# Another order for the first round of the gated layers, and for the loop over attention heads

## The reference

```
u = rms_norm_2(x, norm_w) @ w_in
z_a, xbc, dt_raw, q_b, k_b, v_b, gate_lr, g_b = split_cols(u, EVEN_SPLITS)
xbc = silu(causal_depthwise_conv(xbc, conv_w, conv_b))
...
y_diag = einsum('bcgeij,bcjgep->bcigep', cb[:, :, :, None] * decay_ij, xdt)
y = y_diag + y_off + d_skip[:, :, None] * x_c          # ssd_chunked_scan
y_a = rms_norm_2(y_a * silu(z_a), ssd_norm_w)
...
scores = einsum('bnihd,bnjhd->bnhij', q * exp(gcs - ref), k * exp(ref - gcs))
chunk_kv = einsum('bnjhd,bnjhv->bnhdv', k * exp(g_last[:, :, None] - gcs), v)
o_b = rms_norm_2(gla_chunked(q_b, k_b, v_b, log_decay), gla_norm_w) * silu(g_b)
x = x + concatenate([y_a, o_b]) @ w_out
...
o = moba_attention(q, k, v) * silu(z)                  # softmax attention
x = x + o @ w_out
```

## Time and profile before

| | us |
|---|---|
| median of 3 runs | 868.39 (868.36 to 868.85) |
| the profiled execution | 868.39 |
| its span | 866.6 |
| PE busy | 841.5 (97%) |
| DVE busy | 613.7 (71%) |
| ACT busy | 490.8 (57%) |
| POOL busy | 145.1 (17%) |

### The profile page before, as it was taken

The page is one execution under the profiler, slowest core; times in us unless marked ns, Lnnn a source line. Parts: engine busy times, 40 slices in busy tenths (PEclk is TensorE's granted clock), DMA queues, the critical chain, the costliest instruction groups (busy, mean ns, idle before and its releaser), DMA issues.

```text
span 866.6 us, 16776 instructions
## 1 busy us (share of the span) xinstructions
PE 841.5 (97%) x6768; PEld 803.8 (93%) x6768; DVE 613.7 (71%) x1004; ACT 490.8 (57%) x814; POOL 145.1 (17%) x151
## 2 busy tenths in 40 slices
PE   7999999999999999999999999789999999999996
PEld 6999999999999989999999999789999999888886
DVE  6647787886666686767764478797887697568754
ACT  6345556445444565555564458558777555346654
POOL 0000000000000333333341121335434011000002
PEclk9999999999999999999999999899999999999998
DMA  9654424436666524665566624435544376654431
GB/s 338 210 153 128 158 98 158 135 112 180 192 178 190 175 87 155 194 187 181 174 193 215 191 82 155 163 124 176 183 147 154 115 217 184 186 171 143 123 98 49
DMA packets 39853, 139.81 MB, mean 161 GB/s; under 512 B 4432, under 2 KB 5600, under 8 KB 39648
## 3 DMA queue, kind: packets, MB, share of 16 engines
q1 hardware_dynamic: 37728, 135.71, 49.8%
q10 hardware_dynamic: 2048, 3.02, 1.0%
HBM read 137.65 MB, written 1.06 MB: 160 GB/s over the span
## 4 chain that ended last, share of the span: by engine, by line
PE 79%; DVE 12%; ACT 4%; POOL 3%; issue 1%; DMA 1%; DVEq 0%; SPq 0%; ACTq 0%; POOLq 0%
PE ps L1593 62%; PE ps L1596 5%; DVE weights_lo L984 4%; PE ps L1618 3%; PE ps L1690 1%; DVE arena L1204 1%; DVE arena L1176 1%; PE ps L1680 1%; POOL arena L441 1%; PE ps L1705 1%; PE ps L1960 1%; PE ps L1942 1%; DMA raw_weights<-weights_in 1%; DVE x_lo L1171 1%; POOL arena L462 1%
## 5 line engine op out<-in xcount | busy, mean ns | idle before, releaser
L1593 PE MATMUL ps<-x_hi,weights_hi 128*128 128x256 f32 (+3 forms) x1288 | 374.5, 291 | 6.3 <-DVE x_lo L999 2.8
L984 DVE TENSOR_TENSOR weights_lo<-raw_weights,weights_hi 128x1024 fp32r<-128x1024 f32 x252 | 311.7, 1241 | 92.9 <-ACT weights_hi L549 92.8
L1593 PE MATMUL ps<-x_lo,weights_hi 128*128 128x256 f32 (+3 forms) x1288 | 364.6, 283 | 0.0
L1593 PE MATMUL ps<-x_hi,weights_lo 128*128 128x256 f32 (+3 forms) x1288 | 364.1, 283 | 0.0
L549 ACT ACTIVATE weights_hi<-raw_weights 128x1024 fp32r<-128x1024 f32 x252 | 264.8, 1053 | 163.5 <-issue 71.0
L1593 PEld LDWEIGHTS ps<-x_hi,weights_hi 128*128 128x128 f32 x1288 | 244.1, 190 | 14.3 <-issue 7.0
L1593 PEld LDWEIGHTS ps<-x_lo,weights_hi 128*128 128x128 f32 x1288 | 244.3, 190 | 1.0 <-issue 0.7
L1593 PEld LDWEIGHTS ps<-x_hi,weights_lo 128*128 128x128 f32 x1288 | 244.4, 190 | 0.0
L1593 PE MATMUL ps<-y_hi,weights_hi 128*128 128x256 f32 (+1 forms) x488 | 137.8, 282 | 1.4 <-POOL y_lo L445 1.4
L1593 PE MATMUL ps<-y_lo,weights_hi 128*128 128x256 f32 (+1 forms) x488 | 137.4, 282 | 0.0
L1593 PE MATMUL ps<-y_hi,weights_lo 128*128 128x256 f32 (+1 forms) x488 | 137.1, 281 | 0.0
(11 more groups left out here) (230 smaller groups left out, 1075.0 us busy)
## 6 DMA issues: line engine op xcount, KB each, us to landing
raw_weights<-weights_in SPq DMA_DIRECT2D x252, 512.0 KB, 3.7
arena<-decay_rows ACTq DMA_DIRECT2D x8, 256.0 KB, 3.9
masks<-masks_in SPq DMA_DIRECT2D x1, 1379.0 KB, 11.0
hidden<-xT_in SPq DMA_DIRECT2D x2, 272.0 KB, 3.6
hidden<-xT_in SPq DMA_DIRECT2D x1, 544.0 KB, 6.2
raw_weights<-weights_in SPq DMA_DIRECT2D x2, 256.0 KB, 4.3
out<-arena SPq DMA_DIRECT2D x4, 128.0 KB, 2.2
out<-arena ACTq DMA_DIRECT2D x4, 128.0 KB, 2.1
```

The source lines that it names most:

```text
L984: d.sig(TT(wlo[:, s * CW:(s + 1) * CW], raw[:, (c % RAW) * CW:(c % RAW + 1) * CW], whi[:, s * CW:(s + 1) * CW].bitcast(F32), ALU.subtract) ...
L1593: ins = mm(bank(BANK_OF[no])[:, 0:b - a], wt, x_[:, kt, a:b], start=s0, stop=s1)
```

## The change

Nothing is computed otherwise, and no instruction of weight is added or removed; orders change in two places.

First round of the second layer (p = 0):

- DVE: the convolution of `ex(0)` and the first `decay_sums` come ahead of `take_queries(0)`; `ex(1)` is convolved ahead of `take_keys(0)` and of the `cb` masks. `ssd_y(0)` and `gate_y(0)` move from ahead of `feed(("eg", 0))` to behind `conv_in(("ex", 2))`.
- ACT: the tanh of `ex(0)` and of `ex(1)` come earlier, `feed(("ev", 0))` comes behind the second; `gla_exps(0)` comes right behind `decays(0)`, ahead of `take_values(0)` and of the feeds for `ez(0)` and `eg(0)`; `take_keys(0)` comes earlier.
- POOL: `gla_args(0)` comes ahead of the first `ssd_weights`.
- PE: `turn_x(0)` comes ahead of the projection `eg(0)`; `turn_keys(0)` and `turn_x(1)` ahead of `ez(1)`; `ssd_heads(1)` ahead of `eg(1)`.

Loop over heads of the third layer:

- ACT: `feed(("mq", i))` comes ahead of `soft_exp(i-1)`.
- DVE: within a turn of the loop, the query, the feed, `normalise`, `m_out`, `m_half`, feed, `m_low` and `m_full`, with no part of the gate held over to the next turn.
- PE: `m_scores(0)` comes right behind the projection `mq(0)`, where it was inside `mq(1)`.

The diff, cut to this (lines of the two DVE loops are left out where the rows below show them):

```
@@ gpsimd
             pool.wait_ge(S("cb_taken"), 2)
+            gla_args(0)
             for p in range(4):
                 ssd_weights(2 * p)
-                if p == 0:
-                    gla_args(0)
                 gla_keys(p)
@@ scalar
             tap(("ex", 1), 1, xs[:, 1, :])
+            half_tanh(("ex", 0), xs[:, 0, :])
             feed(("ek", 0))
...
-            feed(("ev", 0))
-            half_tanh(("ex", 0), xs[:, 0, :])
+            half_tanh(("ex", 1), xs[:, 1, :])
...
+            feed(("ev", 0))
             decays(0)
             for p in range(4):
                 u = 2 * p
                 if p:
                     feed(("ek", p))
                     gla_squares(p - 1)
-                    gla_exps(p)
+                gla_exps(p)
+                if p:
                     feed(("ev", p))
                 take_values(p)
...
                 if p == 0:
                     feed(("eg", 0))
-                    gla_exps(0)
-                    half_tanh(("ex", 1), xs[:, 1, :])
...
-                    take_keys(p)
+                take_keys(p)
...
-                if p == 0:
-                    take_keys(0)
...
             for i in range(KT + 1):
                 if i >= 2:
                     prob_copy(i - 2)
+                if i < KT:
+                    feed(("mq", i))
                 if i >= 1:
                     soft_exp(i - 1)
-                if i < KT:
-                    feed(("mq", i))
@@ vector
                 else:
+                    ssd_args(0)
+                    split_lo()
                     z_half(("ez", 0), zs[:, 0, :])
+                    split_lo()
                     feed(("ez", 0))
                     z_half(("eg", 0), gs[:, 0, :])
-                    ssd_y(0)
                 feed(("eg", u))
                 z_full(("ez", u), zs[:, 0, :])
-                gate_y(u)
+                if p:
+                    gate_y(u)
                 z_full(("eg", u), gs[:, u % 4, :])
...
                 if p == 0:
+                    ssd_y(0)
+                    gate_y(0)
                     ssd_args(1)
@@ tensor
                 project(("ez", u), xhi, xlo, META, T)
                 if p:
                     turn_x(u + 1)
+                else:
+                    pe.wait_ge(S("cb_taken"), 2)
+                    turn_x(0)
                 project(("eg", u), xhi, xlo, META, T)
                 if p:
                     turn_keys(p)
-                else:
-                    pe.wait_ge(S("cb_taken"), 2)
-                    turn_x(0)
...
                 if p == 0:
                     ssd_heads(0)
+                    turn_keys(0)
+                    turn_x(1)
                 project(("ez", u + 1), xhi, xlo, META, T)
-                if p:
-                    ssd_heads(u + 1)
-                else:
-                    turn_x(1)
-                    turn_keys(0)
+                ssd_heads(u + 1)
                 project(("eg", u + 1), xhi, xlo, META, T)
-                if p == 0:
-                    ssd_heads(1)
```

More of the change, by code:

```diff
@@ L1290, in take_keys @@
                 d.sig(TT(e_k[:, p % 2, :], r, rL, ALU.mult), "out_taken")
+            take_queries(0)
+            feed(("eq", 0))
+            conv_rest(("ex", 1), 1, xs[:, 1, :])
+            z_full(("ex", 0), xs[:, 0, :], name="xsilu")
+            take_keys(0)
+            feed(("ek", 0))
+            z_full(("ex", 1), xs[:, 1, :], name="xsilu")
+            for g_ in range(2):
+                dve.wait_ge(S("cb_ready"), g_ + 1)
+                d.sig(TT(cb[:, g_, :], bank(4 + g_)[:, 0:CC], mask("causal"), ALU.mult), "cb_taken")
             def z_half(tile, dst):
@@ L1353, in gla_low @@
                           "go_split")
-            take_queries(0)
-            feed(("eq", 0))
-            feed(("ek", 0))
-            conv_rest(("ex", 0), 0, xs[:, 0, :])
-            z_full(("ex", 0), xs[:, 0, :], name="xsilu")
-            for g_ in range(2):
-                dve.wait_ge(S("cb_ready"), g_ + 1)
-                d.sig(TT(cb[:, g_, :], bank(4 + g_)[:, 0:CC], mask("causal"), ALU.mult), "cb_taken")
-            take_keys(0)
-            split_lo()
-            dve.wait_ge(S("tkc_ready"), 1)
-            ssd_args(0)
-            split_lo()
-            decay_sums(0)
-            conv_rest(("ex", 1), 1, xs[:, 1, :])
-            z_full(("ex", 1), xs[:, 1, :], name="xsilu")
+            dve.wait_ge(S("tkc_ready"), 1)
             for p in range(4):
```

73 lines of the change are left out of this document (29 added, 44 removed).

## The result

| | before | changed kernel |
|---|---|---|
| median, us | 868.62 (868.36 to 868.88, 4 runs) | 875.69 (873.93 to 876.32, 4 runs) |
| ratio | | 1.0079, 95% interval 1.0060 to 1.0096 |
| the profiled execution, us | 868.39 | 875.22 |
| its span, us | 866.6 | 873.3 |

What follows compares the result with a forecast made beforehand. The prediction took PE, busy 97% of the span, as the bound. It summed 868.4 + 0.4 (first round) + 5.8 (loop over heads) = 874.6 us, with a range of 870.2 to 877.5.

Steps and rivals of the forecast that it cites:

- The start of the round: First round: `ez(0)` begins at 544.0, 2.7 us later; PE then waits 1.9 us for `turn_x(0)`.
- The middle: First round: tanh of `eg(0)` at 557.2, `ssd_y(0)` done at 559.1, PE idle 3.0 us, POOL's products done at 564.4.
- The end of 559.3: First round: latest end of `ssd_y(0)` by the Trainium skill's rule, with only `z_full` slowed by GpSimd.
- The term: First round's net effect on the time: forecast as +0.4 us, with the clock falling behind the 3.0 us wait.
- Its two values for the round's end: First round ends 2.8 us early if the clock stays at 2.4 GHz, 0.4 us late if it falls.
- a clock that stays up: First round, no clock fall behind the 3.0 us wait: the round ends 2.8 us early instead of 0.4 late.
- The rival of 871.4: First round: the clock does not fall after the 3.0 us wait, or only briefly; 871.4 us, chance 0.24.
- The loop: Loop over heads: `m_turn` waits 0.56 us in each full turn and 1.36 at i = 1; 5.8 us in all.
- DVE's new order costs nothing: Loop over heads: the scores' maximum, nearest to being late, is done 0.7 us before ACT asks; cost nothing.
- Contention on the whole path (877.5): First round: DVE and POOL collide repeatedly, 3 us on PE's path, and the clock stays low; 877.5 us, chance 0.12.
- The loop loses nothing (866.2): Loop over heads: the turns fit, leaving only the first round's gain; 866.2 us, chance 0.07.
- half and half (868.5): Half of the loop's loss and the first round's gain cancel; 868.5 us, chance 0.09.

Runs made afterwards that it cites:

- the first filled round: First-round edits alone plus six unused float32 matmuls ahead of `turn_x(1)`, in the kernel before: 866.81 us against 869.22, ratio 0.9972.
- Filling the gap: Six unused matmuls added ahead of `turn_x(1)`: in the changed kernel 873.54 us, 1.0047 of before; in the kernel with first-round edits alone 866.81 us, 0.9972.
- two kernels: Kernel before with only ACT's split ahead of `soft_exp`: 882.12 us, 1.0144. Changed kernel with that one edit undone: 877.89 us, 1.0098.
- the padded changed kernel: Changed kernel with three unused matmuls in front of each of the 8 `m_turn`: 876.18 us, 1.0075 of before.

## Why the prediction was right, and where not

**The start of the round.** `ez(0)` 2.7 late and begun at 544.0: 2.75 and 544.11. `turn_x(0)` at 548.8 behind a wait of 1.9: 548.71, but without a wait. The prediction left the clock at full speed behind the first idle stretch; it fell there too. It cost next to nothing, since PE would have waited. In the kernel of the first filled round the clock stayed up at this place, and there the wait showed, 1.56 us.

**The middle.** The tanh of `eg(0)` ends at 557.03 (557.2 predicted), POOL's products at 563.68 (564.4). `ssd_y(0)` ends at 559.80, not 559.1: this term was mis-sized. I let DVE stand ready for `z_full(eg(0))` and took one slowed instruction; in fact it came late to `z_full(ez(0))` too, behind a split, and did both while POOL multiplied:

```profile
556.53 2.35 DVE L1248 SCALAR_TENSOR_TENSOR arena<-arena 128x256 f32<-128x256 f32 x2
```

```profile
556.39 2.21 POOL L462 TENSOR_TENSOR arena<-arena 128x384 f32<-128x384 f32 x2 [0.86 <-ACT arena L797]
```

2.35 us for two that take 0.42 each alone (such a row stands in the same timeline, L1248 at 545.50). The rule of the Trainium skill that the prediction weighed (SBUF — State Buffer, "Who interferes with whom") agrees with both rows: these two have two SBUF inputs and were slowed, `ssd_y(0)`, which reads PSUM as well, took 0.47 while POOL worked. The end of 559.3 that I worked out beside it was too early, because I counted one such `z_full`, not two.

The wait came to 3.7 us, not 3.0, the clock fell as forecast, the waits of `gla_scores(0)` and `gla_out(0)` went, and `ex(3)` begins at 569.90 (569.7). The term was +0.4 and is +0.5 in this trace. Two errors met in it: `turn_x(1)` began 0.8 later, and the slow stretch to `ssd_heads(1)` and `eg(1)` cost less than I took. That they met so closely is luck. In three other executions of the same round, in kernels that differ elsewhere, the term is -0.8, -0.8 and -0.4 us, because the clock came back earlier or did not fall the first time; the prediction took one length of the slow stretch, that of before, for all. Its two values for the round's end do not quite follow from its own terms either: 1.5 early and the wait of 1.1 make 2.6, not 2.8, and 1.6 late less 1.1 makes 0.5, not 0.4.

What I gave for a clock that stays up, 3.2 us less, was too much. Filling the gap gained 2.4 in the changed kernel's round and 2.1 to 2.8 in the medians, and 1.2 and 1.8 in the kernel with the first-round edits alone. The rival of 871.4 would have come out near 873.

**The loop.** From the end of `mq(i)` to `m_turn` I had 4.27 us; the rows have 794.11 and 798.38, 4.27. The other terms, with what was measured in brackets: 1.36 at i = 1 (1.36), 0.6 for `m_scores(0)` (0.52), 0.5 at the last `m_attend` (0.5). A turn costs 0.60, not 0.56. Sum 6.0 against 5.8.

**What was wrong in the reason.** "DVE's new order costs nothing" holds beside ACT's new order and not by itself, and the loss does not vanish with ACT's edit, as the prediction's account let one expect: two kernels fell outside what was expected of them. The time came out right because the sum followed the chain through the pair of orders as they stand together. It said nothing about either alone, and I took it to. What it missed is that DVE's new order moves the maxima from 1.7 us ahead of the end of `mq` to 0.25 behind it, and DVE's own split ahead of `normalise`; both are hidden only as long as ACT's exponentials stand behind its split. The maxima come before ACT asks for them, as the prediction had it (794.36 against 795.23).

**Rivals.** Contention on the whole path (877.5): there was contention on the path, at the two `z_full`, and `ssd_y(0)` ended 0.7 us later than forecast. The loop loses nothing (866.2) and half and half (868.5) fell with the turn of 8.93 us. The range of 870.2 to 877.5 held the median, and its runs.

## What to carry to other kernels

An instruction that waits for a later event than its neighbours (here the split that needs the end of `mq(i)`) belongs behind everything that is already ready on its engine; count the chain from that event to the waiting step, and compare it with the work that the waiting engine has left. A step moved ahead of its neighbour on one engine and on the other can be neutral or harmful depending on its partner, so a pair of orders is tested as a pair, and one edit alone is not a share of it. And a wait is not worth its length: behind one, the clock may fall, and what that costs depends on whether the next wait would have taken the time anyway.

## What the hardware showed that was not expected

The same idle stretch did not always have the same effect on TensorE's clock. PE idled 2.72 to 2.75 us ahead of `ez(0)` in every kernel with the first-round edits. In the changed kernel the granted clock fell behind it to 0.50 (the window 546:548 above); in the filled first round it stayed at full speed, with PE idle for the whole of the first of these windows:

```profile
544.00:546.00 2.00, 0.00 (x0) 1.00 0.00 0
546.00:548.00 2.00, 1.57 (x13) 1.00 0.23 45
```

The program is the same in both up to this place. Of the seven traces with this idle stretch the clock fell behind it in five and stayed up in two, this one and that of the padded changed kernel. The Trainium skill (TensorE: Matmul & The Clock Gate, Part 1 on the clock gate) has the moment at which the clock rises vary between runs of one kernel. It says so of a kernel's start; the rows here show a difference of that kind for a fall in the middle. What decides it in a given run these experiments don't show.
